# First attention: causal masks added by VectorE in PSUM, turned probabilities copied by ScalarE, next scores one filler block sooner

## The chip, the cores and the metric

The kernel runs on one core of one Trainium2 chip. The metric is device time in microseconds (us). The time before is the median of 3 runs. The shares, rows and durations come from one profiled execution of the kernel before.

## The reference

Two transformer blocks for one sequence of 512 tokens, width 1024, all in float32. The change touches the attention of the first block ("NSA", 8 heads of 64 dimensions, in 2 key groups). For each block of 128 queries it makes three masked softmaxes: over compressed keys, over selected blocks (at this length all 8 blocks of 64 keys are selected, so the mask is causal), and over a window of 512 (causal too). The three outputs are weighted by gates and added:

```python
s = jnp.einsum('qghd,qgnbd->qghnb', qi, ks) * scale
mask_s = sel_valid[..., None] & (kpos <= t[:, None, None, None])
p_s = masked_softmax(s.reshape(...), mask_s.reshape(...))
...
mask_w = ((wpos[None, :] >= 0) & (diff >= 0) & (diff < WINDOW))[:, None, None, :]
p_w = masked_softmax(s, mask_w)
...
o = g[..., 0:1] * o_c + g[..., 1:2] * o_s + g[..., 2:3] * o_w
```

Beside it the first block has a retention branch, whose input projections (`ret_in`, 16 tiles of 128 outputs) do not depend on the attention. Everything else (gates, merges, two feed-forward layers, a second attention, a state-space scan, cross attention) lies before or behind and is not changed.

## The kernel before

Each large product is `gemm(name, s, ...)`, one weight slot of 1024 rows by 128 outputs. An operand is split in a high and a low part, so each of the 8 row blocks k of a slot is three matmuls of 512 columns (line 1791): high by high, low activation by high weight, high activation by low weight. One such group of three is called a filler block here when it stands inside the attention. ScalarE makes the high part of a weight slot (`split_hi`, line 593), VectorE the low part (`split_lo`, line 1075), three slots ahead.

The attention is a loop over 16 units, u = 4p + i: p is a pair of heads, i a block of 128 queries, and the tile is 128 rows by (i+1)*128 keys, so units of i = 0, 1, 2, 3 have tiles of 128, 256, 384, 512 columns. The order on each engine is written out by hand, and engines meet by semaphores. For unit u:

- TensorE scores: banks 0 and 1 hold the selected branch of the two heads, banks 2 and 3 the window branch, bank 4 the compressed one (lines 1953, 1963). The mask is a matmul too: identity by the mask, added in PSUM to the last 128 columns of each bank (line 1956; line 1961 for the compressed branch).
- VectorE takes the row maxima (lines 1346 to 1354), ScalarE the exponentials (778 to 785), VectorE the sums, reciprocals, gate weights and the scaling of the probabilities (1365 to 1375).
- TensorE turns the scaled probabilities (line 1880 and 1987) into the same banks, runs 2 filler blocks of `ret_in` slot u, waits for the copy of the selected branch (`nsa_sel_t`), and scores unit u+1; between the selected and the window scores it waits for the copy of the window branch of unit u (`nsa_win_t`). Then come the products with the values (1999, 2002, 2004) and the 6 filler blocks that are left.
- The turned probabilities are copied from PSUM by ScalarE for the selected branch (line 790) and by VectorE for the window and the compressed branch (1379, 1381).
- In eight of the units (those of p = 1 and 2 with i = 0, 1, and all four of p = 3) VectorE also rotates a tile of the retention branch: `ret_rotate_halves` (1327, 1328) before it waits for the exponentials, `ret_rotate_sum` (1332, 1334) at the unit's end. ScalarE evacuates one `ret_in` tile in each unit from the second on (`ret_in_leaves`, line 771) and splits one weight slot.

Unit numbers below run from 0 to 15; a bank is one of the eight parts of PSUM.

Of the kernel before, what the change touches and what calls it, by code (L numbers as in the profile page):

```python
# [9 lines left out]
F32R = mybir.dt.float32r  # L10
ACT = mybir.ActivationFunctionType
ALU = mybir.AluOpType
AX = mybir.AxisListType.X

P = 128
S = 512
SC = S // P
D = 1024
DK = D // P
# [8 lines left out]
NSA_PAIRS = NSA_HEADS // 2  # L28
NSA_SCALE = DH ** -0.5
CMP_LEN, CMP_STRIDE, CMP_HIDDEN = 32, 16, 256  # L30
N_CMP = (S - CMP_LEN) // CMP_STRIDE + 1
# [166 lines left out]
def block_program(nc, xT, mem_t, w_all, params, consts, rope, decay, w_gate, w_dt, w1k, w1v, w2k, w2v, out_t):  # L198
    ctx = ExitStack()
    with ctx:  # L200
        sems = {}

        def sem(name):
            if name not in sems:
                sems[name] = ctx.enter_context(nc.semaphore(name))
            return sems[name]
# [22 lines left out]
        def place(name, shape, off, dt=F32):  # L229

            size = int(np.prod(shape[1:])) * 4
            assert arena0 + off * 1024 + size <= arena_end, (name, off, size, (arena_end - arena0) / 1024)
            return nc.alloc_sbuf_tensor_at(name, shape, dt, offset=arena0 + int(off * 1024))
# [5 lines left out]
        def const(name):  # L239
            return CO[:, CCOL[name][0]:CCOL[name][1]]  # L240

        ACC = [ctx.enter_context(nc.psum_tensor(f"acc{b}", [P, S], F32)) for b in range(2)]
        PS = [ctx.enter_context(nc.psum_tensor(f"bank{b}", [P, S], F32)) for b in range(6)]


        HH = place("act_hi", [P, DK, S], 0, F32R)
# [36 lines left out]
        IDR = place("ident_r", [P, P], 113.5, F32R)  # L283
        CAR = place("causal_r", [P, P], 114, F32R)
        CMR = place("cmp_mask_r", [P, SC * 32], 114.5, F32R)
# [297 lines left out]
        def _(act):  # L583
            A = nc.scalar.activation
# [167 lines left out]
            A(IDR[:], ident, ACT.Copy)  # L752
            A(CAR[:], const("causal"), ACT.Copy)
            A(CMR[:], const("cmp_mask"), ACT.Copy).then_inc(sem("nsa_masks"), 1)
# [18 lines left out]
            for p in range(NSA_PAIRS):  # L773
                for i in range(SC):
# [14 lines left out]
                    for hh in range(2):  # L789
                        ins = A(PTS[:, hh, 0:i + 1, :], PS[hh][:, 0:kw].rearrange("p (c t) -> p c t", t=P), ACT.Copy)  # L790
                    ins.then_inc(sem("nsa_sel_t"), 1)
                    if i:
                        ret_in_leaves(p, i - 1)
                    elif p:
                        act.wait_ge(sem("nsa_pv"), p * SC)
                        A(OA[:, p - 1, :], PS[5][:], ACT.Copy).then_inc(sem("nsa_out"), 1)
                        ret_in_leaves(p - 1, 3)
# [264 lines left out]
        def _(dve):  # L1062
# [273 lines left out]
            def rotated_at(p, i):  # L1336
# [3 lines left out]
                return (p - 1, i) if p and i < 2 else None  # L1340

            for p in range(NSA_PAIRS):
                for i in range(SC):
                    u, kw = p * SC + i, (i + 1) * P
                    dve.wait_ge(sem("nsa_sel_scored"), u + 1)
                    V.reduce_max(MX[:, 2:3], PS[0][:, 0:kw], AX)
                    chain.link(V.reduce_max(MX[:, 3:4], PS[1][:, 0:kw], AX))
                    TS(NM[:, 2:4], MX[:, 2:4], -NSA_SCALE, None, ALU.mult).then_inc(sem("nsa_sel_max"), 1)
                    dve.wait_ge(sem("nsa_win_scored"), u + 1)
                    V.reduce_max(MX[:, 0:2], PS[4][:, 0:64].rearrange("p (h c) -> p h c", h=2)[:, :, 0:N_CMP], AX)  # L1350
                    V.reduce_max(MX[:, 4:5], PS[2][:, 0:kw], AX)
# [5 lines left out]
                    turned = rotated_at(p, i)  # L1357
                    if turned:
                        ret_rotate_halves(*turned)

                    dve.wait_ge(sem("nsa_exp"), u + 1)
# [14 lines left out]
                        sem("nsa_win_scaled"), 1)  # L1376

                    dve.wait_ge(sem("nsa_win_turned"), u + 1)
                    V.tensor_copy(PTC[0:N_CMP], PS[4][0:N_CMP, P:3 * P].rearrange("p (h t) -> p h t", h=2))
                    for hh in range(2):  # L1380
                        ins = V.tensor_copy(PTW[:, hh, 0:i + 1, :], PS[2 + hh][:, 0:kw].rearrange("p (c t) -> p c t", t=P))
                    ins.then_inc(sem("nsa_win_t"), 1)
                    if turned:
# [374 lines left out]
        def _(pe):  # L1758
# [190 lines left out]
            def wide_scores(p, i, branch):  # L1949

                kw = (i + 1) * P
                for hh, rows in enumerate(head_rows):
                    MM(PS[2 * branch + hh][:, 0:kw], QK[rows, p, i * P:(i + 1) * P], QK[rows, 5 + branch, 0:kw], start=True,  # L1953
                       stop=False)
                for hh in range(2):
                    ins = MM(PS[2 * branch + hh][:, i * P:kw], IDR[:], CAR[:], start=False, stop=True)
                return ins
# [17 lines left out]
            for p in range(NSA_PAIRS):  # L1975
                for i in range(SC):
                    u, cols = p * SC + i, slice(i * P, (i + 1) * P)

                    pe.wait_ge(sem("nsa_sel_scaled"), u + 1)
# [8 lines left out]
                    ins.then_inc(sem("nsa_win_turned"), 1)  # L1988
                    gemm("ret_in", u, HH, HL, ks=range(0, 2))
                    pe.wait_ge(sem("nsa_sel_t"), u + 1)  # L1990
# [14 lines left out]
                    ins.then_inc(sem("nsa_pv"), 1)  # L2005
                    gemm("ret_in", u, HH, HL, ks=range(2, DK))

# [485 lines left out]
```

## Time and profile before

| what | value |
|---|---|
| median of 3 runs | 2032.09 us (2030.95 to 2032.53) |
| profiled execution | 2032.29 us, span of the trace 2030.6 us |
| TensorE busy over the span | 1981.5 us, 98% |
| VectorE busy | 1140.7 us, 56% |
| ScalarE busy | 812.5 us, 40% |
| attention loop, first score to last filler block | about 99.6 to 290.2 us of the span |

Times in rows count from the start of the span. A matmul row gives its start and its duration; durations overlap, since matmuls are pipelined, so what a matmul costs is the distance from its start to the next start. One float32 matmul stands as two records.

### The profile page before, as it was taken

What the parts mean: (1) busy time and instruction counts of PE and PEld (TensorE: products, weight loads), DVE (VectorE), ACT (ScalarE), POOL (GpSimd) and SP (SyncE); (2) the same over time, 40 slices, a digit from 0 to 9 for tenths busy, and PEclk for the clock granted to TensorE, in tenths of its full rate; (3) what the DMA queues carried; (4) which work ended last, traced back from release to release, by engine and by line L of the source; (5) the groups of instructions that cost most, each with busy time, mean ns of one, the idle gap of its engine ahead of it and who ended that gap; (6) DMA issues with size and microseconds to landing.
All of it is one profiled execution on the core that took longest, in us unless ns stands there. A gap on an engine that the chain in (4) does not pass through costs nothing.

```text
span 2030.6 us, 25955 instructions
## 1 busy us (share of the span) xinstructions
PE 1981.5 (98%) x10494; PEld 1607.2 (79%) x10494; DVE 1140.7 (56%) x1837; ACT 812.5 (40%) x1365; POOL 111.2 (5%) x131
## 2 busy tenths in 40 slices
PE   8999999999999999999999999999999999999997
PEld 6767767788888888888877777888889788888886
DVE  5567766644456444422627888796564465444323
ACT  4144432533344222222427777554435443222321
POOL 0000000000011000000200000331010020000000
PEclk9999999999999999999999999999999999999999
DMA  7111112233322333333222221113223223333331
GB/s 276 55 32 53 42 52 63 73 96 91 104 83 92 95 94 94 89 96 96 83 78 70 63 63 52 53 42 93 84 90 119 90 78 94 94 93 94 94 95 61
DMA packets 49431, 170.55 MB, mean 84 GB/s; under 512 B 5520, under 2 KB 8080, under 8 KB 48928
## 3 DMA queue, kind: packets, MB, share of 16 engines
q1 hardware_dynamic: 48816, 166.73, 27.4%
q0 software_dynamic: 496, 2.16, 0.3%
q8 instruction: 83, 1.36, 0.3%
q14 instruction: 36, 0.29, 0.0%
HBM read 166.77 MB, written 2.10 MB: 83 GB/s over the span
## 4 chain that ended last, share of the span: by engine, by line
PE 90%; DVE 7%; issue 1%; ACT 1%; DMA 0%; SPq 0%; DVEq 0%
PE acc L1791 57%; PE bank L1791 18%; PE bank L1880 2%; PE bank L1953 1%; PE bank L2092 1%; PE acc L2296 1%; DVE w_lo L1075 1%; PE bank L2127 1%; PE bank L2029 1%; DVE bank L1155 1%; PE bank L1926 1%; PE bank L2283 1%; PE bank L2317 1%; DVE residual L1161 1%; PE bank L1813 1%
## 5 line engine op out<-in xcount | busy, mean ns | idle before, releaser
L1075 DVE TENSOR_TENSOR w_lo<-w_raw,w_hi 128x1024 fp32r<-128x1024 f32 (+2 forms) x306 | 365.8, 1198 | 302.6 <-ACT w_hi L593 302.1
L1791 PE MATMUL acc<-act_hi,w_hi 128*128 128x512 f32 (+1 forms) x1160 | 457.5, 394 | 17.4 <-DVE w_lo L1075 9.7
L1791 PE MATMUL acc<-act_lo,w_hi 128*128 128x512 f32 (+1 forms) x1160 | 445.4, 384 | 0.0
L1791 PE MATMUL acc<-act_hi,w_lo 128*128 128x512 f32 (+1 forms) x1160 | 445.3, 384 | 0.0
L593 ACT ACTIVATE w_hi<-w_raw 128x1024 fp32r<-128x1024 f32 (+2 forms) x306 | 314.7, 1030 | 211.6 <-PE acc L1791 181.0
L1791 PEld LDWEIGHTS acc<-act_hi,w_hi 128*128 128x128 f32 x1160 | 218.9, 189 | 71.9 <-issue 16.3
L1791 PEld LDWEIGHTS acc<-act_hi,w_lo 128*128 128x128 f32 x1160 | 218.9, 189 | 47.0
L1791 PEld LDWEIGHTS acc<-act_lo,w_hi 128*128 128x128 f32 x1160 | 219.1, 189 | 45.7 <-issue 2.2
L1791 PE MATMUL bank<-act_hi,w_hi 128*128 128x512 f32 (+1 forms) x520 | 192.6, 370 | 1.2 <-DVE w_lo L1075 1.2
L1791 PE MATMUL bank<-act_lo,w_hi 128*128 128x512 f32 (+1 forms) x520 | 191.0, 367 | 0.0
L1791 PE MATMUL bank<-act_hi,w_lo 128*128 128x512 f32 (+1 forms) x520 | 191.0, 367 | 0.0
L1791 PE MATMUL acc<-ffn_hi,w_lo 128*128 128x512 f32 (+1 forms) x352 | 134.2, 381 | 0.0
L1791 PE MATMUL acc<-ffn_lo,w_hi 128*128 128x512 f32 (+1 forms) x352 | 134.2, 381 | 0.0
L1791 PE MATMUL acc<-ffn_hi,w_hi 128*128 128x512 f32 (+1 forms) x352 | 134.2, 381 | 0.0
L1791 PEld LDWEIGHTS bank<-act_hi,w_hi 128*128 128x128 f32 x520 | 97.8, 188 | 19.5 <-DVE w_lo L1075 1.4
L1791 PEld LDWEIGHTS bank<-act_lo,w_hi 128*128 128x128 f32 x520 | 97.8, 188 | 17.9 <-issue 0.2
L1791 PEld LDWEIGHTS bank<-act_hi,w_lo 128*128 128x128 f32 x520 | 97.8, 188 | 17.7
L617 ACT ACTIVATE ffn_hi<-product 128x512 fp32r<-128x512 f32 x44 | 27.8, 633 | 195.5 <-DVE product L1480 195.5
L1121 DVE TENSOR_TENSOR square_sum<-square_sum,evacuated 128x512 f32<-128x512 f32 (+1 forms) x47 | 31.1, 662 | 99.8 <-ACT evacuated L634 99.7
L1791 PEld LDWEIGHTS acc<-ffn_lo,w_hi 128*128 128x128 f32 x352 | 66.2, 188 | 14.2
L1791 PEld LDWEIGHTS acc<-ffn_hi,w_hi 128*128 128x128 f32 x352 | 66.2, 188 | 14.1
L1791 PEld LDWEIGHTS acc<-ffn_hi,w_lo 128*128 128x128 f32 x352 | 66.2, 188 | 13.9
(453 smaller groups left out, 3015.5 us busy)
## 6 DMA issues: line engine op xcount, KB each, us to landing
w_raw<-w_all SPq DMA_DIRECT2D x282, 512.0 KB, 3.6
w_raw<-w_all SPq DMA_DIRECT2D x16, 384.0 KB, 3.2
residual<-xT SPq DMA_DIRECT2D x8, 256.0 KB, 7.8
cmp_w_k<-w1k SPq DMA_DIRECT2D x1, 2048.0 KB, 8.3
cmp_w_v<-w1v SPq DMA_DIRECT2D x1, 2048.0 KB, 12.5
w_raw<-w_all SPq DMA_DIRECT2D x8, 256.0 KB, 2.6
out_t<-residual SPq DMA_DIRECT2D x16, 128.0 KB, 1.7
ret_decay<-decay POOLq DMA_DIRECT2D x4, 256.0 KB, 3.4
```

The lines of the kernel that those rows point to most:

```text
L593: A(WH[:, c % HI_RING, 0:nb * P], WR[:, c % RAW_RING, 0:nb * P], ACT.Copy).then_inc(s_hi, 1)
L617: A(dst, PR[:, j % 2, 0:n], ACT.Copy).then_inc(s_ph, 1)
L1075: TT(WL[:, c % RAW_RING, 0:nb * P], WR[:, c % RAW_RING, 0:nb * P], WH[:, c % HI_RING, 0:nb * P].bitcast(F32), ALU.subtract).then_inc(s_lo, 1)
L1121: TT(SSQ[:, cols], SSQ[:, cols], ev(name, m)[:, cols], ALU.add).then_inc(s_fsq, 1)
L1155: STT(out=scaled_at(k), in0=FO[:, k, cols], scalar=factor, in1=PS[(4, 3)[h]][:, cols], op0=ALU.mult, op1=ALU.mult).then_inc(sem("branch_sc ...
L1161: TT(X[:, k, cols], X[:, k, cols], scaled_at(k), ALU.add).then_inc(s_x, 1)
L1791: ins = MM(bank[:, cols], w[:, at, k * P:(k + 1) * P], x, start=first and r == 0 and k == 0, stop=last and r == 2 and k == nb - 1)
L1813: ins = MM(bank[:, c * P:(c + 1) * P], RC[:, c:c + 1].broadcast_to([P, P]), ident, start=True, stop=True)
L1880: ins = TR(PS[bank][:, to + c * P:to + (c + 1) * P], src[:, c * P:(c + 1) * P], ident)
L1926: ins = MM(PS[n][:, j * 2 * N_CMP:(j + 1) * 2 * N_CMP], W1[t][:, b, j * P:(j + 1) * P], BLK[t][:, b, :], start=b == 0, stop=b == 15)
L1953: MM(PS[2 * branch + hh][:, 0:kw], QK[rows, p, i * P:(i + 1) * P], QK[rows, 5 + branch, 0:kw], start=True, stop=False)
L2029: ins = MM(PS[3 + e][:, j * P:S], RVT[:, j, e * P:(e + 1) * P], RSM[:, j, 0:S - j * P], start=j == 0, stop=j == SC - 1)
```

## The change

Three things change. The four mask matmuls of each unit (line 1956) go, and with them the rounded copy of the mask; VectorE adds the mask to the last 128 columns of each of the four banks instead, two adds before the maxima of each branch. The copies of the turned window and compressed probabilities move from VectorE to ScalarE, right behind those of the selected branch. In the units with i below 3, the next scores begin after 1 filler block in place of 2 (i = 3: 2 as before, and 3 in the very last unit); the blocks behind them grow from 6 to 7. VectorE's rotation now stands as a whole at the end of the unit.

```diff
@@ act
             A(IDR[:], ident, ACT.Copy)
-            A(CAR[:], const("causal"), ACT.Copy)
@@
                     ins.then_inc(sem("nsa_sel_t"), 1)
+                    act.wait_ge(sem("nsa_win_turned"), u + 1)
+                    for hh in range(2):
+                        A(PTW[:, hh, 0:i + 1, :], PS[2 + hh][:, 0:kw].rearrange("p (c t) -> p c t", t=P), ACT.Copy)
+                    A(PTC[0:N_CMP], PS[4][0:N_CMP, P:3 * P].rearrange("p (h t) -> p h t", h=2), ACT.Copy).then_inc(
+                        sem("nsa_win_t"), 1)
                     if i:
                         ret_in_leaves(p, i - 1)
@@ dve
+            def hide_later(bank, i):
+
+                block = PS[bank][:, i * P:(i + 1) * P]
+                return TT(block, block, const("causal"), ALU.add)
+
             for p in range(NSA_PAIRS):
                 for i in range(SC):
                     u, kw = p * SC + i, (i + 1) * P
                     dve.wait_ge(sem("nsa_sel_scored"), u + 1)
+                    hide_later(0, i)
+                    chain.link(hide_later(1, i))
                     V.reduce_max(MX[:, 2:3], PS[0][:, 0:kw], AX)
...
                     dve.wait_ge(sem("nsa_win_scored"), u + 1)
+                    hide_later(2, i)
+                    chain.link(hide_later(3, i))
...
                     turned = rotated_at(p, i)
-                    if turned:
-                        ret_rotate_halves(*turned)
-
                     dve.wait_ge(sem("nsa_exp"), u + 1)
...
-                    dve.wait_ge(sem("nsa_win_turned"), u + 1)
-                    V.tensor_copy(PTC[0:N_CMP], PS[4][0:N_CMP, P:3 * P].rearrange("p (h t) -> p h t", h=2))
-                    for hh in range(2):
-                        ins = V.tensor_copy(PTW[:, hh, 0:i + 1, :], PS[2 + hh][:, 0:kw].rearrange("p (c t) -> p c t", t=P))
-                    ins.then_inc(sem("nsa_win_t"), 1)
+                    if turned:
+                        ret_rotate_halves(*turned)
                     if turned:
                         ret_rotate_sum(*turned)
@@ pe
                 for hh, rows in enumerate(head_rows):
-                    MM(PS[2 * branch + hh][:, 0:kw], QK[rows, p, i * P:(i + 1) * P], QK[rows, 5 + branch, 0:kw], start=True,
-                       stop=False)
-                for hh in range(2):
-                    ins = MM(PS[2 * branch + hh][:, i * P:kw], IDR[:], CAR[:], start=False, stop=True)
+                    ins = MM(PS[2 * branch + hh][:, 0:kw], QK[rows, p, i * P:(i + 1) * P], QK[rows, 5 + branch, 0:kw],
+                             start=True, stop=True)
                 return ins
@@
+                    lead = 1 if i < SC - 1 else 2 if p < NSA_PAIRS - 1 else 3
...
-                    gemm("ret_in", u, HH, HL, ks=range(0, 2))
+                    gemm("ret_in", u, HH, HL, ks=range(0, lead))
...
-                    gemm("ret_in", u, HH, HL, ks=range(2, DK))
+                    gemm("ret_in", u, HH, HL, ks=range(lead, DK))
```

TensorE at the end of unit 0's turning, in the kernel before: the last filler block ahead of unit 1's scores, those scores with their masks, and the first product with the values.

```order
L1791 MATMUL acc0<-act_hi_50,w_hi 128x512
L1791 MATMUL acc0<-act_lo_51,w_hi 128x512
L1791 MATMUL acc0<-act_hi_50,w_lo_49 128x512
L1953 MATMUL bank0<-nsa_qk_58 128x256
L1953 MATMUL bank1<-nsa_qk_58 128x256
L1956 MATMUL bank0<-causal_r_89,ident_r_88 128x128
L1956 MATMUL bank1<-causal_r_89,ident_r_88 128x128
L1953 MATMUL bank2<-nsa_qk_58 128x256
L1953 MATMUL bank3<-nsa_qk_58 128x256
L1956 MATMUL bank2<-causal_r_89,ident_r_88 128x128
L1956 MATMUL bank3<-causal_r_89,ident_r_88 128x128
L1961 MATMUL bank4<-cmp_mask_r_90,ident_r_88 128x64
```

The same place in the kernel after, from the turn of unit 0's compressed probabilities on.

```order
L1991 MATMUL bank4<-const_cols,cmp_probs_79 31x128 x2
L1796 MATMUL acc0<-act_hi_50,w_hi 128x512
L1796 MATMUL acc0<-act_lo_51,w_hi 128x512
L1796 MATMUL acc0<-act_hi_50,w_lo_49 128x512
L1958 MATMUL bank0<-nsa_qk_58 128x256
L1958 MATMUL bank1<-nsa_qk_58 128x256
L1958 MATMUL bank2<-nsa_qk_58 128x256
L1958 MATMUL bank3<-nsa_qk_58 128x256
L1964 MATMUL bank4<-cmp_mask_r_89,ident_r_88 128x64
L1966 MATMUL bank4<-cmp_keys_70,nsa_qk_58 128x64
```

The four mask matmuls are gone, and one filler block stands between the turning and the scores where two stood.

VectorE at the end of unit 4 (p = 1, i = 0) and the start of unit 5, in the kernel before: scaling, copies of the turned probabilities, the second half of the rotation, and the maxima.

```order
L1374 TENSOR_SCALAR nsa_probs_78<-nsa_probs_78,nsa_weights_87 128x128
L1375 TENSOR_TENSOR cmp_probs_79<-cmp_probs_79,nsa_weights_87 128x2x31
L1379 COPY cmp_probs_t_82<-bank4 31x256
L1381 COPY win_probs_t_81<-bank2 128x128
L1381 COPY win_probs_t_81<-bank3 128x128
L1332 TENSOR_TENSOR tmp_b_54<-evacuated,ret_rope_table_61 128x512
L1334 TENSOR_TENSOR ret_qk_94<-tmp_a_53,tmp_b_54 128x512
L1346 TENSOR_REDUCE nsa_max_83<-bank0 128x1
L1347 TENSOR_REDUCE nsa_max_83<-bank1 128x1
L1348 TENSOR_SCALAR nsa_neg_max_84<-nsa_max_83 128x2
L1350 TENSOR_REDUCE nsa_max_83<-bank4 128x2
```

The same place in the kernel after.

```order
L1384 TENSOR_TENSOR cmp_probs_79<-cmp_probs_79,nsa_weights_87 128x2x31
L1330 TENSOR_TENSOR tmp_a_53<-evacuated,ret_rope_table_61 64x512
L1331 TENSOR_TENSOR tmp_a_53<-evacuated,ret_rope_table_61 64x512
L1335 TENSOR_TENSOR tmp_b_54<-evacuated,ret_rope_table_61 128x512
L1337 TENSOR_TENSOR ret_qk_93<-tmp_a_53,tmp_b_54 128x512
L1348 TENSOR_TENSOR bank0<-bank0,const_cols 128x128
L1348 TENSOR_TENSOR bank1<-bank1,const_cols 128x128
L1356 TENSOR_REDUCE nsa_max_83<-bank0 128x1
L1357 TENSOR_REDUCE nsa_max_83<-bank1 128x1
L1358 TENSOR_SCALAR nsa_neg_max_84<-nsa_max_83 128x2
L1348 TENSOR_TENSOR bank2<-bank2,const_cols 128x128
L1348 TENSOR_TENSOR bank3<-bank3,const_cols 128x128
```

The three copies have left VectorE, all four operations of the rotation stand together behind the scaling, and each pair of maxima has two adds ahead of it.

ScalarE in unit 1 of the kernel after: the three copies stand between those of the selected branch and the evacuation of the `ret_in` tile.

```order
L788 ACTIVATE sel_probs_t_80<-bank0 128x256
L788 ACTIVATE sel_probs_t_80<-bank1 128x256
L792 ACTIVATE win_probs_t_81<-bank2 128x256
L792 ACTIVATE win_probs_t_81<-bank3 128x256
L793 ACTIVATE cmp_probs_t_82<-bank4 31x256
L769 ACTIVATE evacuated<-acc0 128x512
L592 ACTIVATE w_hi<-w_raw 128x1024
```

In the kernel before, the evacuation follows the two copies of the selected branch at once.

## Rows read from the trace of the kernel before

**Rows 1.** The page: busy time by engine, and the chain that ended last.

```profile
PE 1981.5 (98%) x10494; PEld 1607.2 (79%) x10494; DVE 1140.7 (56%) x1837; ACT 812.5 (40%) x1365; POOL 111.2 (5%) x131
PE 90%; DVE 7%; issue 1%; ACT 1%; DMA 0%; SPq 0%; DVEq 0%
```

**Rows 2.** Busy time by stretch; PEclk is TensorE's granted clock.

```profile
core 0: us, PE busy (x) PEld busy (x) DVE busy (x) ACT busy (x) POOL busy (x), PEclk, DMA share, GB/s
100.00:112.00 12.00, 8.16 (x35) 5.79 (x33) 4.67 (x23) 3.36 (x13) 0.00 (x0) 0.57 0.01 1
112.00:292.00 180.00, 177.84 (x1174) 132.38 (x1173) 129.44 (x364) 75.81 (x215) 0.70 (x1) 1.00 0.16 47
```

**Rows 3.** Timeline of TensorE, scores of unit 7: start us, us.

```profile
178.88 0.44 PE L1956 MATMUL bank<-causal_r,ident_r 128*128 128x128 f32 x2
179.25 1.13 PE L1953 MATMUL bank<-nsa_qk 64*128 64x512 f32 x4
180.31 0.44 PE L1956 MATMUL bank<-causal_r,ident_r 128*128 128x128 f32 x2
180.59 0.24 PE L1961 MATMUL bank<-cmp_mask_r,ident_r 128*128 128x64 f32 x1
```

**Rows 4.** Groups by shape, VectorE and ScalarE: count, busy us, mean ns.

```profile
L1556 DVE TENSOR_TENSOR bank<-bank,const_cols 128x256 f32<-128x256 f32 x24 | 8.7, 420 | 0.0
...
L1556 DVE TENSOR_TENSOR bank<-bank,const_cols 128x128 f32<-128x128 f32 x16 | 3.9, 289 | 0.0
```

**Rows 5.** Timeline of unit 7, VectorE, then TensorE's turn.

```profile
179.36 0.69 DVE L1346 TENSOR_REDUCE nsa_max<-bank 128x1 f32<-128x512 f32 x1 [1.48 <-PE bank L1956]
...
181.12 0.22 DVE L1350 TENSOR_REDUCE nsa_max<-bank 128x2 f32<-128x62 f32 x1 [0.27 <-PE bank L1963]
...
186.22 0.48 DVE L1372 TENSOR_SCALAR nsa_probs<-nsa_probs,nsa_weights 128x512 f32<-128x512 f32 x1
...
187.13 1.91 PE L1880 MATMUL bank<-const_cols,nsa_probs 128*128 128x128 f32 x16
```

**Rows 6.** Timeline of TensorE, turns of units 1 and 5.

```profile
118.10 1.04 PE L1880 MATMUL bank<-const_cols,nsa_probs 128*128 128x128 f32 x8
...
162.64 0.40 PE L1791 MATMUL acc<-act_lo,w_hi 128*128 128x512 f32 x1
162.87 0.40 PE L1791 MATMUL acc<-act_hi,w_lo 128*128 128x512 f32 x1
163.51 1.31 PE L1880 MATMUL bank<-const_cols,nsa_probs 128*128 128x128 f32 x8 [0.24 <-DVE nsa_probs L1372]
```

**Rows 7.** Timeline of unit 5, ScalarE and VectorE.

```profile
160.07 0.46 ACT L785 ACTIVATE cmp_probs<-bank,nsa_neg_max 128x31 f32<-128x31 f32 x2
...
160.28 0.69 DVE L1327 TENSOR_TENSOR tmp_a<-evacuated,ret_rope_table 64x512 f32<-64x512 f32 x1
...
160.98 0.69 DVE L1328 TENSOR_TENSOR tmp_a<-evacuated,ret_rope_table 64x512 f32<-64x512 f32 x1
...
161.70 0.22 DVE L1365 TENSOR_TENSOR cmp_probs<-cmp_probs,const_cols 128x62 f32<-128x62 f32 x1
```

**Rows 8.** Timeline of TensorE, turns and value product of the last units.

```profile
266.56 1.66 PE L1880 MATMUL bank<-const_cols,nsa_probs 128*128 128x128 f32 x12 [0.20 <-DVE nsa_probs L1372]
279.41 2.01 PE L1880 MATMUL bank<-const_cols,nsa_probs 128*128 128x128 f32 x16 [0.16 <-DVE nsa_probs L1372]
283.44 1.09 PE L1999 MATMUL bank<-sel_probs_t,sel_values 128*64 128x128 f32 x16 [0.38 <-DVE win_probs_t L1381]
```

**Rows 9.** Timeline, unit 0.

```profile
100.02 0.66 PE L1956 MATMUL bank<-causal_r,ident_r 128*128 128x128 f32 x2
100.61 0.80 PE L1953 MATMUL bank<-nsa_qk 64*128 64x128 f32 x4
...
101.33 0.69 PE L1956 MATMUL bank<-causal_r,ident_r 128*128 128x128 f32 x2
...
106.50 1.21 PE L1880 MATMUL bank<-const_cols,nsa_probs 128*128 128x128 f32 x4 [3.84 <-DVE nsa_probs L1372]
```

**Rows 10.** Timeline, end of units 7 and 5: copies, and the next maximum.

```profile
163.90 0.22 DVE L1375 TENSOR_TENSOR cmp_probs<-cmp_probs,nsa_weights 128x62 f32<-128x62 f32 x1
...
167.69 0.56 DVE L1346 TENSOR_REDUCE nsa_max<-bank 128x1 f32<-128x384 f32 x1 [0.20 <-PE bank L1956]
...
188.20 1.08 ACT L790 ACTIVATE sel_probs_t<-bank 128x512 f32<-128x512 f32 x2 [3.56 <-PE bank L1880]
```

More of the change, by code:

```diff
@@ L283, in block_program @@
         IDR = place("ident_r", [P, P], 113.5, F32R)
-        CAR = place("causal_r", [P, P], 114, F32R)
         CMR = place("cmp_mask_r", [P, SC * 32], 114.5, F32R)
```

## The prediction

> **What bounds the kernel now.** I read the page first. TensorE is busy 98% of the span and makes 90% of the chain that ended last, VectorE 7% [rows 1]. So a microsecond is saved where TensorE issues less or stops waiting, and a microsecond of VectorE counts only where TensorE waits for it. Then the stretches: in the attention loop behind its start TensorE is busy 177.84 of 180 us, at full clock, with VectorE at 129.44 and ScalarE at 75.81 [rows 2]. VectorE is the second engine, at 72%; ScalarE has room. In the first 12 us the granted clock is 0.57, so most of it is at 1.2 in place of 2.4 GHz. Last the timelines of single units, for what each part costs from start to start and for where TensorE stands still.
>
> **Part 1, the mask matmuls.** In unit 7 the selected pair starts at 178.88 and the next scores at 179.25: 0.37 us. The window pair starts at 180.31 and the next row at 180.59: 0.28 us [rows 3]. The mask pairs have 128 columns whatever the tile, so these two hold for all units; together 0.65. The 0.09 between the two is the way back from whole-array to half-array matmuls. The first pair disappears with its switches. Behind the second a whole-array matmul follows anyway (line 1961), which then meets the switch itself; for this I keep 0.05 of the 0.09 in the sum: 0.60 a unit, bounds 0.56 and 0.65. Units 1 to 15 are scored at full clock: 15 x 0.60 = 9.0 us (8.4 to 9.75). Unit 0 is counted in part 4. The Trainium skill (TensorE: Matmul & The Clock Gate, Back-to-back issue gap) has about 81 ns for a matmul of 128 columns with its weight load in a sustained stream; by that the 60 matmuls are worth 4.9 us and the whole would end 4.1 us later, near 2024; the rows here, with their switches, have 0.14 to 0.19 each, and I go by them.
>
> **Part 2, what the adds put on the path.** An add of a constant to 128 columns in PSUM stands in the trace in another stage at 289 ns [rows 4]; a second follows, by the 0.20 us spacing of the small operations, so a pair with its link (0.04) is 0.20 + 0.29 + 0.04 = 0.53 us, two pairs 1.06. The next larger form, 256 columns, has 420 ns: the upper bound, 0.79 a pair. Are they hidden? The cover is TensorE's work between the scores and the turn. Take unit 7, the widest tile. Window scores begin at 179.25, and the turn at 187.13 [rows 3, 5]: 7.88 us. After, that is 0.23 less (window masks) and one filler block more. A block is three matmuls at 0.23 [rows 6], 0.70, so 8.35. VectorE: from its first maximum at 179.36 to the end of the second scaling, 186.22 + 0.48 = 186.70, are 7.34 us [rows 5]. It grows by 1.06, and loses the 0.27 that it waited for the window scores: 8.13. With 0.11 ahead and 0.04 for the semaphore that is 8.28 against 8.35: slack 0.07, where it was 0.39. So the units with i = 3 just fit. The same subtraction gives 0.30 for i = 2 and 0.5 for i = 1; with i = 0 no block is gained, but the tile is the smallest and 1 us or more is left. I charge 0.1 us of waiting for each of the four widest units, 0.4 in all. Without the extra block each unit of i = 1 to 3 would stand worse by 0.70: that is what the earlier scores buy.
>
> **Part 3, the waits that go.** Unit 5 (i = 1, with rotation) turns at 163.51, 0.64 after the last filler matmul where the spacing is 0.23: 0.41 late; inside the turn it waits again, 1.31 against the 1.04 of unit 1, which has no rotation: 0.27 [rows 6]. Units 9 and 13 repeat it: 3 x 0.68 = 2.04. Unit 14 shows 0.20 idle, unit 15 0.16, and 0.17 of each wait is hidden in the length of the row (0.40 duration, 0.23 spacing): 0.37 and 0.33; with the waits inside the turn 0.56 and 0.43. Behind the last turn the value product waits 0.38 for VectorE's copies [rows 8]. Together 3.4 us. All of it comes from VectorE. The halves of the rotation, 0.70 each, lie between the exponentials, which end at 160.07 + 0.46 = 160.53, and the sums at 161.70 [rows 7]; behind the unit they free 1.13 us of path, so unit 5 has -0.41 + 1.13 + 0.47 - 0.68 = +0.5 slack (0.47: block less masks; 0.68: adds less the idle before the window maximum). The copies of the last unit go to ScalarE.
>
> What is late next? The rotation, now four operations of about 0.70, 2.8 us, between the last scaling and the next scores. In unit 5 that gap is from 163.90 + 0.22 to 167.69, 3.57 us [rows 10]; it loses a block (0.70) and the selected masks (0.37), and gains 0.5 since the turn no longer waits, less the 0.27: 2.7. So VectorE is late by some 0.1 us there, which the 0.3 of unit 6 takes. In units 4, 8 and 12 (i = 0) and behind unit 14 TensorE comes to the next scores later against VectorE's last scaling, so more is left. ScalarE: in unit 7 its two copies end at 188.20 + 1.08 = 189.28, as the turned window is ready; two more (1.08) and the small one (bound by one wide copy, 0.6; I take 0.35) end near 190.7, and the window scores of unit 8 stand behind two blocks (1.40) and the first scores (about 0.4, half of the 0.72 at half clock in unit 0), from 187.13 + 1.91 = 189.04: 190.9 [rows 5, 9, 10]. Slack 0.2. With narrower tiles the copies shrink as fast as the turn. Behind them on ScalarE are the evacuation and the split for slot u+3, later by about 1.4 us; VectorE's split that needs it stands behind the next unit's window maxima, and the accumulator is wanted a unit later. TensorE's weight slots are used in the same order, so SyncE's loads and the decay table's load on GpSimd only move along with them; DMA is at 16% [rows 2].
>
> **Part 4, unit 0.** At half clock the mask pairs take 100.61 - 100.02 = 0.59 and about 0.49, and the turn waits at 106.50 [rows 9]. TensorE is idle there, so only the path counts: window scores ready 1.08 sooner, adds 0.53 more, and VectorE busy with the selected branch until then; 0.46 us sooner. Work issued in that gap runs at half clock as long as the slow stretch lasts, so 0.25 of it is kept (0 to 0.46).
>
> **Sum.** 9.0 + 3.4 + 0.25 - 0.4 = 12.2 us. The profiled execution took 2032.29 us, 1.7 more than its span, and gives 2020.1; the median is 0.2 lower: **2019.9 us**. Its own range has 8.4 to 9.75 for the masks, 2.5 to 3.5 for the waits, and 0 to 2 for new waits: 2018.3 to 2022.
>
> **The rivals.**
> *The adds are dearer* (chance 0.15). At the price of the 256-column form each unit's path grows by 0.52 more: i = 3 waits 0.45, i = 2 0.22, times four is 2.7, and the rotating units, already level, add about 1. The time is 2023.6. For it: between filler blocks VectorE would be busy almost without a pause in units 5, 9, 13 to 15. Against: the row of the same shape.
> *A longer slow stretch* (0.06). TensorE's idle gap in unit 0 begins a microsecond earlier and ends half a microsecond earlier, so it is longer. If the clock came back later by as much again as the slow stretch lasts now (0.57 over 12 us is 10.3 us at half rate), 5.1 us are lost: 2025.0. Against: the same work follows as before, sooner. The Trainium skill (TensorE: Matmul & The Clock Gate, HAM oscillation — how this bites in real kernels) says that idle gaps between bursts of matmuls put the clock back to half rate, so a longer gap speaks for this rival; the trace agrees that the gap and the slow stretch lie together.
> *Hardly any change* (0.05): masks at the low price and three waits of 0.1 to 0.5 us in every four units, within 4.1 us of before, about 2028.5.
> *Slower* (0.04): VectorE becomes the bound. TensorE's slack over four units is about 0.07 + 0.3 + 0.5 + 1.4 = 2.3 us; 12.2 us lost over four rounds are 3.05 each, so the path must grow by (3.05 + 2.3) / 4 = 1.3 a unit, 0.33 an add: from 0.53 us an add in place of 0.20 the gain is gone, and from 0.6 the kernel is slower by over 0.2%, 2037 at 0.62. For it: VectorE would write to PSUM while TensorE writes to it and ScalarE reads it, and each add would have to suffer as much. Against: the add at 289 ns stands in a stage where those two work as well.
>
> **How the numbers follow.** The forecast has 0.70. A measurement tells about 0.2% (4.1 us) from no change. Above 2025.5 I leave about 0.1, below 2018.3 about 0.06; so 2018.3 to 2025.5. Faster: 0.70 + 0.15 + 0.06 is 0.91, I take 0.90; same 0.06; slower 0.04.
>
> **What would show it.** Scores to scores without a gap, 0.6 us a unit less on TensorE; adds at 0.29; no wait of TensorE at the turns with i = 1 and 2, some hundredths at i = 3; the window scores never waiting for ScalarE; VectorE late for the maxima behind units 5, 9 and 13 by 0.1. Turns late by more than 0.3 at i = 3, or a clock below 0.57 in the first 12 us, would make it wrong.

## The result and the profile after

The changed kernel takes 2017.62 us (median of 4 runs, 2016.59 to 2019.11) against 2032.31 us for the kernel before (4 runs, 2030.95 to 2032.83): ratio 0.9931, 95% interval 0.9918 to 0.9944. It is 14.7 us faster, where 12.2 were forecast, and the time lies 0.7 us below the range (2018.3 to 2025.5).

The page of the kernel after, its busy times and its chain, answers to [rows 1].

```profile
PE 1967.8 (98%) x10430; PEld 1599.1 (79%) x10430; DVE 1136.9 (56%) x1853; ACT 828.9 (41%) x1412; POOL 111.3 (6%) x131
...
PE 92%; DVE 6%; issue 1%; ACT 1%; DMA 0%; SPq 0%; DVEq 0%
```

TensorE is busy 13.7 us less over the span. Its share of the chain that ended last rose from 90 to 92%, and VectorE's fell from 7 to 6%. Busy time by stretch in the kernel after, columns as in [rows 2]:

```profile
100.00:112.00 12.00, 7.62 (x39) 5.20 (x38) 6.71 (x32) 4.99 (x20) 0.00 (x0) 0.60 0.01 1
112.00:275.00 163.00, 163.00 (x1092) 123.24 (x1090) 122.65 (x370) 89.56 (x256) 0.70 (x1) 1.00 0.17 51
275.00:400.00 125.00, 123.36 (x515) 92.47 (x515) 78.41 (x102) 45.29 (x67) 1.62 (x3) 1.00 0.24 70
```

The loop ends 15 us sooner, and by these rows TensorE is busy in all of it (some waits don't show in them, see below). The slow stretch is as long as before: from 97 to 112 us, which holds the whole of it in both traces, the granted clock is 0.66 before and after, about 10.2 us at half rate. It begins and ends some 0.6 us sooner, and so the window from 100 us on reads 0.60 where it read 0.57. Behind the loop nothing moved: from the first matmul that turns retention values (290.86 before, 275.81 after) to the end of the span are 1739.7 and 1740.1 us.

Where the time came from, by the starts of TensorE's rows in both traces:

| stretch | before | after | gained |
|---|---|---|---|
| start of the span to the first scores | 99.60 | 99.20 | 0.40 |
| first scores to the turn of unit 1 | 18.50 | 17.26 | 1.24 |
| turn of unit 1 to the first turned retention value | 172.76 | 159.35 | 13.41 |
| from there to the end | 1739.7 | 1740.1 | -0.4 |

The first and the last row cancel. The edit changes only one thing in them, the copy of the mask on ScalarE ahead of the first scores, and with that copy back (e1 below) the first scores start at 99.16. Over the fourteen traces told of here the first scores start between 98.8 and 99.9 and the last stretch takes 1739.7 to 1741.0, so about half a microsecond either way is what any one trace has of its own. In the two longest last stretches (e10 and e11) the clock falls to half for 6.8 us near 1246 us, where the other traces have 3.4 us in that part of the kernel.

TensorE in unit 7 of the kernel after, timeline, from the last filler matmul to the value products; [rows 3] are the same unit before.

```profile
170.89 0.40 PE L1796 MATMUL acc<-act_hi,w_lo 128*128 128x512 f32 x1
171.22 1.99 PE L1958 MATMUL bank<-nsa_qk 64*128 64x512 f32 x8
173.13 0.30 PE L1964 MATMUL bank<-cmp_mask_r,ident_r 128*128 128x64 f32 x1
173.27 0.41 PE L1966 MATMUL bank<-cmp_keys,nsa_qk 128*128 128x64 f32 x2
173.61 0.66 PE L2003 MATMUL bank<-sel_probs_t,sel_values 128*64 128x128 f32 x8
```

And the same unit before, a few rows around those shown ahead:

```profile
174.81 1.47 PE L1880 MATMUL bank<-const_cols,nsa_probs 128*128 128x128 f32 x12
...
176.26 0.47 PE L1791 MATMUL acc<-act_hi,w_hi 128*128 128x512 f32 x1
...
177.83 1.13 PE L1953 MATMUL bank<-nsa_qk 64*128 64x512 f32 x4
...
180.67 0.41 PE L1963 MATMUL bank<-cmp_keys,nsa_qk 128*128 128x64 f32 x2
181.01 0.33 PE L1999 MATMUL bank<-sel_probs_t,sel_values 128*64 128x128 f32 x2
```

From the first score to the first value product: 181.01 - 177.83 = 3.18 us before, 173.61 - 171.22 = 2.39 after. That is 0.79, not 0.60. The scores row alone shows where the difference lies: from the first of its eight records to the next row are 173.13 - 171.22 = 1.91 us, where before each group of four took 1.05 (177.83 to 178.88) and again 1.06, and 1.91 is 0.2 less than the two. The same 0.79 holds for every tile width in the loop: 1.91 to 1.12 where the unit scored has i = 0, 2.76 to 1.97 at i = 2. (One float32 score product is two passes, a record each, and the records of the two heads start 0.01 us apart; so eight records are four passes, with two heads in each.)

The turns of units 6 and 7 after, timeline of TensorE:

```profile
168.48 0.40 PE L1796 MATMUL acc<-act_hi,w_lo 128*128 128x512 f32 x1
168.71 1.65 PE L1885 MATMUL bank<-const_cols,nsa_probs 128*128 128x128 f32 x12
...
170.34 0.48 PE L1796 MATMUL acc<-act_hi,w_hi 128*128 128x512 f32 x1
...
180.21 0.40 PE L1796 MATMUL acc<-act_hi,w_lo 128*128 128x512 f32 x1
180.50 2.02 PE L1885 MATMUL bank<-const_cols,nsa_probs 128*128 128x128 f32 x16
...
182.49 0.48 PE L1796 MATMUL acc<-act_hi,w_hi 128*128 128x512 f32 x1
```

No row shows idle time, and still TensorE waits a little. A turn with i = 2, from its first record to the next filler matmul, takes 1.45 us when nothing is late (unit 6 before: 176.26 - 174.81); here it is 170.34 - 168.71 = 1.63, 0.18 more. With i = 3 it takes 1.88; here it begins 0.06 late (0.29 behind the last filler matmul, where 0.23 is the spacing) and takes 1.99, 0.11 more. Read this way, over units 1 to 15, the waits at the turns are 1.22 us after and 3.04 before, and before the last value product waited 0.45 more.

### The profile page after: what moved, and what is told of

The parts are those of the page before. It is cut to its first block, busy times and chain, and to the rows that moved or that the text cites. A ratio compares the mean times of both kernels' runs of the same rounds, so it can differ in the third digit from the quotient of the medians.

```text
span 2015.9 us, 25890 instructions
## 1 busy us (share of the span) xinstructions
PE 1967.8 (98%) x10430; PEld 1599.1 (79%) x10430; DVE 1136.9 (56%) x1853; ACT 828.9 (41%) x1412; POOL 111.3 (6%) x131
## 4 chain that ended last, share of the span: by engine, by line
PE 92%; DVE 6%; issue 1%; ACT 1%; DMA 0%; SPq 0%; DVEq 0%
PE acc L1796 58%; PE bank L1796 18%; PE bank L1885 2%; PE bank L2096 1%; PE acc L2300 1%; PE bank L1958 1%; PE bank L2131 1%; PE bank L2033 1%; DVE bank L1158 1%; PE bank L1931 1%; DVE w_lo L1078 1%; PE bank L2287 1%; PE bank L2321 1%; DVE residual L1164 1%; PE bank L1818 1%
## 5 line engine op out<-in xcount | busy, mean ns | idle before, releaser
L852 ACT ACTIVATE evacuated<-evacuated 128x512 f32<-128x512 f32 x44 | 27.9, 633 | 121.3 <-DVE evacuated L1479 121.3
```

The costliest lines, as they stand in the source:

```text
L852: A(ev(up, t), ev(up, t), ACT.Silu).then_inc(sem("gate_made"), 1)
```

## The experiments

The method for all of them: the loop is measured from the turn of unit 1 to the first turned retention value, waits are turns that begin or end later than the same turn without a wait, and "score stage" is the distance from the first score of a unit with i = 2 to the value product that follows. The kernel before was measured beside each group of kernels again: 2031.7 us with e1 to e4, 2031.9 with e5 to e8, 2032.6 with e9 to e12; the ratios go by these.

| kernel | median us | loop us | waits at turns us | score stage us |
|---|---|---|---|---|
| before | 2032.3 | 172.76 | 3.04 | 2.76 |
| after | 2017.6 | 159.35 | 1.22 | 1.97 |
| all masks on TensorE (e1) | 2029.2 | 169.26 | 0 | 2.76 |
| selected masks on TensorE (e2) | 2024.0 | 166.12 | 0 | 2.54 |
| window masks on TensorE (e3) | 2019.3 | 161.31 | 0 | 2.19 |
| no masks (e4) | 2016.0 | 158.27 | 0 | 1.97 |
| adds alone (e5) | 2030.7 | 172.68 | 13.56 | 1.97 |
| lead of two blocks (e6) | 2024.6 | 166.68 | 8.53 | 1.97 |
| rotation split (e7) | 2021.6 | 163.56 | 5.36 | 1.97 |
| copies on VectorE (e8) | 2036.9 | 175.75 | 16.30 | 1.97 |
| after again (e9) | 2018.2 | 159.33 | 1.16 | 1.97 |
| no compressed mask (e10) | 2016.9 | 159.01 | 2.30 | 1.86 |
| two matmuls ahead (e11) | 2016.5 | 158.28 | 0 | 1.97 |
| both (e12) | 2015.6 | 157.27 | 0.61 | 1.86 |

**What the mask matmuls cost: e1, e2, e3.** In the changed kernel, mask matmuls are put back for both branches, for the selected one, or for the window one, and VectorE's adds for them go.

```diff
                     ins = MM(PS[2 * branch + hh][:, 0:kw], ...,
-                             start=True, stop=True)
+                             start=True, stop=not (branch == 0))
+                if branch == 0:
+                    for hh in range(2):
+                        ins = MM(PS[2 * branch + hh][:, i * P:kw], IDR[:], CAR[:], start=False, stop=True)
@@ dve
-                    hide_later(0, i)
-                    chain.link(hide_later(1, i))
```

(Shown for e2; e1 has `branch in (0, 1)` and no adds, e3 `branch == 1` and no adds to banks 2 and 3. ScalarE's rounded copy of the mask comes back in all three.)

> The changed kernel with all four mask matmuls back on TensorE and no adds on VectorE. Theory S (switches): in the trace of the kernel after, scores to the next product took 0.79 us less per unit than before, because the two middle passes of the scores stand 0.32 apart in place of 0.42 once no whole-array matmul lies between the branches; the masks then cost 15 x 0.79 = 11.9 us, the waits at the turns with i = 2 and 3 (about 1.3 us in the kernel after) vanish, and the time is near 2017.6 + 10.6 = 2028.2. Rival P (the prediction's size, 0.60 a unit, the rest of the gain from elsewhere): 2017.6 + 9.0 - 1.3 = 2025.3.

> The changed kernel with the mask matmuls of the selected branch alone back on TensorE; VectorE adds only the window masks. Theory S: the selected pair costs its own 0.36 and 0.1 on each of the two passes beside it, 0.57 a unit, 8.6 us, less the waits of 1.3: 2024.9, with passes 0.42 apart again in both branches. Rival P: 0.37 a unit, 5.6 less 1.3: 2021.9, passes stay 0.32 apart.

> The changed kernel with the mask matmuls of the window branch alone back on TensorE. Both theories have 0.23 a unit for this pair (a whole-array matmul follows anyway): 3.4 us less the waits of 1.3, 2019.7. Theory S adds that the middle passes stay at 0.32; if they go to 0.42 here, and not with the selected masks, S is wrong.

Measured: 2029.17 us (ratio to before 0.9987, interval 0.9977 to 0.9996), 2024.04 (0.9964, 0.9951 to 0.9977) and 2019.28 (0.9936, 0.9921 to 0.995). Theory S had 2028.2, 2024.9 and 2019.7, at most 1.0 off; rival P was 3.9 us off for e1 and 2.1 for e2. Unit 7 of e2, timeline of TensorE:

```profile
174.53 1.13 PE L1958 MATMUL bank<-nsa_qk 64*128 64x512 f32 x4
175.59 0.44 PE L1962 MATMUL bank<-causal_r,ident_r 128*128 128x128 f32 x2
175.96 1.13 PE L1958 MATMUL bank<-nsa_qk 64*128 64x512 f32 x4
177.02 0.30 PE L1967 MATMUL bank<-cmp_mask_r,ident_r 128*128 128x64 f32 x1
177.15 0.41 PE L1969 MATMUL bank<-cmp_keys,nsa_qk 128*128 128x64 f32 x2
```

Unit 7 of e3, the same view:

```profile
172.70 1.99 PE L1958 MATMUL bank<-nsa_qk 64*128 64x512 f32 x8
174.62 0.44 PE L1962 MATMUL bank<-causal_r,ident_r 128*128 128x128 f32 x2
174.89 0.25 PE L1967 MATMUL bank<-cmp_mask_r,ident_r 128*128 128x64 f32 x1
174.97 0.41 PE L1969 MATMUL bank<-cmp_keys,nsa_qk 128*128 128x64 f32 x2
```

Compare the distance from the first score to the product with the compressed keys: 2.05 us in the kernel after (173.27 - 171.22), 2.62 in e2, 2.27 in e3. The selected pair costs 0.57, the window pair 0.22, and 0.79 are both. The same two matmuls of 128 columns are 2.6 times dearer in the one place. In e2 the scores stand in two groups of 1.06 us, in e3 in one of 1.92. Between the two score groups the pair brings its own 0.37, and it also breaks up a row of four passes over the same half-array layout, of which the two in the middle then take 0.1 more each. e1 has no waits at the turns either, so the waits of before are gone by the other parts of the change, with the masks still on TensorE.

**What the adds cost: e4.** The four adds are taken out of the changed kernel and nothing stands in their place.

```diff
-                    hide_later(0, i)
-                    chain.link(hide_later(1, i))
...
-                    hide_later(2, i)
-                    chain.link(hide_later(3, i))
```

> The changed kernel without the four adds and without mask matmuls: the causal mask of the selected and the window branch is left out of the computation, the rest is the same. It prices the adds on the path. Theory S: TensorE waits about 1.3 us in the loop at the turns with i = 2 and 3 and some 0.5 us of unit 0's gap belong to the adds: 2016.0. Rival D (the adds are hidden everywhere): 2017.6, no change. Rival E (VectorE still sets much of the loop): 2013 or lower.

This kernel leaves the causal mask of two branches out, so it prices the adds and is no version to use. Measured: 2015.99 us (0.992, 0.9905 to 0.9934), as theory S had it. The loop is 1.08 us shorter and all waits at the turns are gone; from the first scores to the turn of unit 1 another 0.38 is saved (17.26 to 16.88). That is the whole price, some 1.5 us, of 64 adds of 0.29 us each, 15.8 us of VectorE's time:

```profile
L1348 DVE TENSOR_TENSOR bank<-bank,const_cols 128x128 f32<-128x128 f32 x64 | 15.8, 293 | 27.5 <-PE bank L1958 27.4
```

(This is the group by shape of the kernel after.) They are hidden but for 1.1 us in the loop and 0.4 ahead of it.

**What hides the adds: e5 to e8.** e5 is the kernel before with the mask edit alone. e6, e7 and e8 each undo one other part of the changed kernel.

```diff
@@ e6
-                    lead = 1 if i < SC - 1 else 2 if p < NSA_PAIRS - 1 else 3
+                    lead = 2
@@ e7
                     turned = rotated_at(p, i)
+                    if turned:
+                        ret_rotate_halves(*turned)
                     dve.wait_ge(sem("nsa_exp"), u + 1)
...
-                    if turned:
-                        ret_rotate_halves(*turned)
                     if turned:
                         ret_rotate_sum(*turned)
@@ e8, dve (and the three copies of act go)
+                    dve.wait_ge(sem("nsa_win_turned"), u + 1)
+                    V.tensor_copy(PTC[0:N_CMP], ...)
+                    for hh in range(2):
+                        ins = V.tensor_copy(PTW[:, hh, 0:i + 1, :], ...)
+                    ins.then_inc(sem("nsa_win_t"), 1)
                     if turned:
                         ret_rotate_halves(*turned)
```

> The kernel before with the masks moved to VectorE and nothing else of the change. Theory H (the other edits are what hides the adds): TensorE issues 11.9 us less, but the adds lengthen VectorE's path by 1.06 in every unit where the slack was 0.4 to 0.7, and in the rotating units there was none; from the slacks the waits grow by 10 to 12 us, so the time is 2030 to 2033. Rival A (the parts add up): 2032.3 - 11.9 + 2 = 2022.

> The changed kernel with 2 filler blocks ahead of the scores in every unit, as before. Theory H: in each of the eleven units with i = 1 to 3 whose scores now come one block earlier the cover falls by 0.70 us against slacks of 0.0 to 0.5: waits of 0.2 to 0.8, together 6 to 8 us, 2023.5 to 2025.5. Rival A: the slack of VectorE is enough, 2017.6 to 2018.5.

> The changed kernel with the halves of the rotation back ahead of the wait for the exponentials. Theory H: 1.1 us of path come back in units 5, 9, 13 (slack 0.5), 14 and 15 (slack 0.1 to 0.3) and none in the four with i = 0: waits of 0.6 to 0.9 in five units, 3 to 4 us, 2020.6 to 2021.6. Rival A: 2017.6.

> The changed kernel with the copies of the turned window and compressed probabilities back on VectorE, ahead of the rotation. Theory H: VectorE has to wait for the turn before it may rotate, and in the rotating units it is then 2 us late for the next maxima; from the slacks 12 to 15 us are lost, 2030 to 2033, all in the units with rotation, next to nothing in units 1 to 4 and 7 to 8. Rival A (VectorE is busy 75% of the loop and has room for 1.1 us a unit): 2018 to 2020.

Measured: e5 2030.66 us (0.9992, 0.9983 to 1.0002), e6 2024.61 (0.9959, 0.9944 to 0.9974), e7 2021.58 (0.9944, 0.9929 to 0.9959), e8 2036.89 (1.0021, 1.0012 to 1.0031). Theory H holds in e5, e6 and e7; in e8 its mechanism shows, but the median is 4 us beyond its range. Rival A is out by 4 to 17 us. What TensorE waited for in the loop by the list of waits, the largest row of each, with total, times and longest (it counts idle time alone); first e5, then e6, e7 and e8:

```profile
PE bank L1887 <- DVE nsa_probs L1379: 9.4, 11, 1.4
```

```profile
PE bank L1885 <- DVE nsa_probs L1381: 3.8, 8, 0.6
```

```profile
PE bank L1885 <- DVE nsa_probs L1383: 2.8, 5, 0.6
```

```profile
PE bank L1885 <- DVE nsa_probs L1376: 12.4, 7, 2.0
```

In e5 the turns of units 5, 9, 13, 14 and 15 are 1.7 us late each, the others with i = 3 0.9, with i = 2 0.7 to 0.8, and the sum is 13.6 us. Of these 3.0 were there before; the 10.5 that are new eat nearly all of the 11.1 that TensorE saves in the loop. In e6 every turn with i = 1, 2, 3 is late, by 0.57, 0.71 and 0.86. In e7 five turns are, beside the 0.16 at i = 3 that the changed kernel has too: 1.0 in units 5, 9, 13, 0.93 in 14, 0.88 in 15. In e8 they are those of units 5, 6, 9, 10, 13, 14 and 15, by 1.9 to 3.1; the others, 0.16 at most.

The 3.1 of unit 14 in e8 is not waiting alone:

```profile
266.22 2.33 PE L1885 MATMUL bank<-const_cols,nsa_probs 128*128 128x128 f32 x12 [1.96 <-DVE nsa_probs L1376]
```

(timeline of TensorE). In this trace the granted clock falls to half once inside the loop, from 266.9 us on for 3.4 us (0.72 over 266 to 272), and the turn takes 2.4 us where 1.64 is usual; TensorE had been busy 9.26 of the 11 us before 266. No other trace here has this. The traced execution is the fastest of ten, 2033.84 us at a mean clock of 0.994, 0.8 above theory H's range; the other nine took 2035.1 to 2037.9 at 0.991 to 0.993. More stretches at half clock in them would account for the rest, but that is not shown, since they left no trace.

So no part gains in proportion to what it takes off an engine; each counts by the turns at which VectorE is late.

**What is left: e9 to e12.** e10 takes out the last mask matmul. e11 moves the boundary by one matmul instead of a block of three; `gemm` gets a range of single matmuls (`steps`).

```diff
@@ e10
-                MM(PS[4][:, 0:64], IDR[:], CMR[:, i * 32:(i + 1) * 32]..., start=True, stop=False)
-                return MM(PS[4][:, 0:64], QK[:, p, i * P:(i + 1) * P], ..., start=False, stop=True)
+                return MM(PS[4][:, 0:64], QK[:, p, i * P:(i + 1) * P], ..., start=True, stop=True)
@@ e11
-                    lead = 1 if i < SC - 1 else 2 if p < NSA_PAIRS - 1 else 3
+                    lead = 2 if i < SC - 1 else 6 if p < NSA_PAIRS - 1 else 9
-                    gemm("ret_in", u, HH, HL, ks=range(0, lead))
+                    gemm("ret_in", u, HH, HL, steps=(0, lead))
-                    gemm("ret_in", u, HH, HL, ks=range(lead, DK))
+                    gemm("ret_in", u, HH, HL, steps=(lead, 3 * DK))
```

In e10 and e12 the maximum of the compressed branch goes over all keys, masked ones too; the exponentials are multiplied by the 0/1 mask as before. It is a bound from above, which keeps its accuracy as long as no masked score lies far above the others.

> The changed kernel itself once more, on the same chip as the next three. Both theories: 2017.6 within 1 us of the earlier median; turns with i = 3 late by 0.17 and those behind units 5, 9, 13 by 0.18 again.

> The changed kernel without the mask matmul of the compressed branch. The maximum is then taken over all compressed keys; the probabilities are multiplied by the 0/1 mask afterwards as before. Theory S: this matmul is the one that meets the way back to the whole array behind the window scores (0.13 to the next start, where 0.08 stood when the window masks were ahead of it), and the next one inherits the switch: 0.08 a unit, 1.2 us. Rival P (it costs its whole distance): 0.13 a unit, 2.0 us. In the trace the first product with the compressed keys then shows 0.19 (S) or 0.14 (P) to its second pass.

> The changed kernel with two filler matmuls ahead of the scores in place of a whole block of three, in units with i below 3: 0.23 us more cover behind them. Theory H: the waits at the turns, 1.2 us in the loop, go, and ScalarE's copies still arrive (the window copies with at most 0.1 to spare at i = 1): 1.0 to 1.2 us faster than the changed kernel. Rival W (the copies come late): the window scores wait 0.1 to 0.2 a unit and the gain is nil or a loss.

> Both edits together: no mask matmul of the compressed branch, and two filler matmuls ahead of the scores. Theory: they add, 1.2 + 1.1 = 2.3 us faster than the changed kernel, 2015.3. Rival W: the copies are the next limit and only one of the two counts.

Measured, on one chip: e9 2018.21 us (2017.06 to 2019.06; ratio to before 0.9931, 0.9919 to 0.9944), e10 2016.87 (2016.09 to 2018.31; 0.9926, 0.9914 to 0.9938), e11 2016.45 (2016.26 to 2017.6; 0.9924, 0.9912 to 0.9937), e12 2015.62 (2015.14 to 2017.25; 0.9921, 0.9908 to 0.9935). The medians are too close for a verdict between neighbours; the loops in the traces are not: 159.33, 159.01, 158.28, 157.27.

Unit 7 of e10, timeline of TensorE:

```profile
171.00 1.99 PE L1958 MATMUL bank<-nsa_qk 64*128 64x512 f32 x8
172.92 0.43 PE L1964 MATMUL bank<-cmp_keys,nsa_qk 128*128 128x64 f32 x2
173.29 0.88 PE L2001 MATMUL bank<-sel_probs_t,sel_values 128*64 128x128 f32 x12
```

From first score to value product 2.29 in place of 2.39: 0.11 a unit at i = 2 (0.10 here), between the 0.08 and the 0.13 of the two theories. The product's own first pass takes 0.16 to the second, where it took 0.14: some 0.02 of a switch is inherited, not 0.05. Of the 1.6 us that 15 units save, 1.1 come back as waits (1.16 to 2.30), since VectorE's path starts at the selected scores, which are not sooner, and its cover is 0.1 shorter; its loop gains 0.32. In e11 every wait at a turn is gone, 1.05 us, and no window score waits for ScalarE, so rival W is out. With both, the loop is 2.06 us shorter than in e9, and 0.6 of waits are left. That is less than the 2.3 expected, and more than 0.32 and 1.05 together: the two matmuls take up 1.7 of the 2.3 that e10 waits. e12 is the fastest version here, 2.6 us by the medians under the changed kernel on the same chip.

## Why the prediction was wrong, step by step

**What bounds the loop** was right: every kernel's loop is TensorE's own work and what it waits at the turns. The loop of e1 (no adds, no waits) less that of e4 (no masks, no waits) is 10.99 us, 14 score stages at 0.79 = 11.06.

**Part 1 failed in size, and by it the time fell below the range.** The step is "together 0.65 ... 0.60 a unit, bounds 0.56 and 0.65", and with it "15 x 0.60 = 9.0 us". It measured 0.79 a unit, 11.1 us in the 14 units scored in the loop and 11.9 if unit 1 is counted alike, and the upper bound, 9.75, was below it. It took the distance from the mask pair to the next row as all that the pair costs. e2 and e3 show what stands in its place: the window pair costs 0.22, as that step had it (0.23), and the selected pair 0.57, where it had 0.37, because it lies between two groups of half-array matmuls and the two passes beside it take 0.1 longer each, inside the score rows. The rows shown ahead already had the length of those score groups; I did not ask what they would be without a break. This one step is 2.9 us (2.7 in the loop alone), more than the whole error of 2.5; the waits of part 2 offset 0.8 of it.

The four mask matmuls of a unit took 0.79 us here, 0.20 each. The figure of the Trainium skill (TensorE: Matmul & The Clock Gate, Back-to-back issue gap), about 81 ns in a sustained stream, would have been further off than mine.

**Part 2 was right in mechanism and too cheap.** The adds cost 293 ns, as the row of the same shape said, and almost all are hidden. I charged 0.4 us of waits; there are 1.22: 0.17 in each of the four units with i = 3 (0.1 was charged), and 0.18, 0.16 and 0.18 behind the rotation in units 6, 10 and 14, where I had VectorE 0.1 late and 0.3 of slack. The subtraction went to the start of the turn alone. In unit 7 that start is 0.06 late where 0.07 of slack was forecast, 0.13 off. The rest is lost inside the turn, which waits a second time, for the scalings of the window branch: 0.11 in unit 7 and all 0.18 in unit 6, whose turn begins on time (168.71 - 168.48 = 0.23). Of these 0.18, 0.13 stand at that second wait, where two starts are 0.19 and 0.16 apart instead of 0.11. The sum had no term for that.

**Part 3 was right.** The waits of before were 3.49 us (3.04 at the turns, 0.45 at the last value product; 3.4 forecast), and all are gone, in e1 as well, where there are no adds. e7 and e8 show that with the adds in place both the moved rotation and ScalarE's copies are needed for it; what either would do without the adds no run shows. ScalarE is in time: the copies end at 184.11 in unit 7,

```profile
181.63 1.09 ACT L788 ACTIVATE sel_probs_t<-bank 128x512 f32<-128x512 f32 x2 [3.25 <-PE bank L1885]
182.78 1.09 ACT L792 ACTIVATE win_probs_t<-bank 128x512 f32<-128x512 f32 x2
183.75 0.36 ACT L793 ACTIVATE cmp_probs_t<-bank 31x256 f32<-31x256 f32 x1
```

with 0.36 us for the small one (0.35 forecast), and the window scores, some 0.3 us behind the first at 184.06, start without a gap.

**Part 4**: the stretch from the first scores to the turn of unit 1 is 1.24 us shorter; with 0.79 taken for unit 1's masks, as in the loop, 0.45 is left for unit 0 where 0.25 was taken, within its bounds. This 0.45 is a remainder and not a reading. What the rows show is that the turn of unit 0 comes 0.68 us sooner after the first scores (6.22 in place of 6.90), where 0.46 was forecast; the terms given for that, 1.08 less 0.53, make 0.55, and 0.46 can't be worked out from them. The other 0.56 is gained behind that turn. There unit 1's scores now begin at 108.26, inside the slow stretch, where they began at 110.51, behind it. So its stage fell from 2.33 to 2.24 us only, against 1.54 in unit 5 at full clock, and the filler block that ran at half clock in its place, 1.30 us, now runs at full clock, 0.70.

The sum for the loop, where every term is read from rows: 14 x 0.79 + 3.49 - 1.22 = 13.3, against 13.41 from the stretches. With unit 1's 0.79 and the remainder it is 11.85 + 3.49 - 1.22 + 0.45 = 14.6, where the forecast had 9.0 + 3.4 - 0.4 + 0.25. The slow end of the forecast's own range, 2022, does not follow from its bounds either: 8.4 + 2.5 - 2 is 8.9 us less, about 2023.2.

**The rivals.** The adds are not dearer than their row (293 against 289 ns). The slow stretch did not grow: it lasts about 10.2 us in both traces, though TensorE's gap in it grew from 3.84 to 4.38 us,

```profile
105.42 1.21 PE L1885 MATMUL bank<-const_cols,nsa_probs 128*128 128x128 f32 x4 [4.38 <-DVE nsa_probs L1381]
```

(timeline of the kernel after, unit 0). The stretch ends 3.8 us behind the turn of unit 0 before and 4.3 behind it after, so half a microsecond more of work ran at half clock, some 0.25 us, an estimate, of the 0.68 that the turn came sooner. The rule of the Trainium skill on idle gaps (TensorE: Matmul & The Clock Gate, HAM oscillation — how this bites in real kernels), which spoke for that rival, did not show here as a later return of the clock.

The slower outcome, VectorE as the bound, is real as a mechanism: e8 is there, at 2036.9 (2033.8 in its trace), by leaving 1 us of copies a unit on VectorE. It needed no dearer adds.

## What to carry to other kernels

- A small matmul between two groups of half-array matmuls costs its own distance and what it does to its neighbours. Ask what the rows beside it would look like without it, and look in the trace for an uninterrupted group; where an add or a multiply by a mask can go elsewhere, take the one first that breaks such a group.
- Work moved to a second engine is free only at the places where the first engine arrives later than it. Write the slack of each unit down, since a part that gains nothing alone (e5) counts together with the others, and ask of every wait inside a stage, not only of the one at its start.
- Waits below the difference between a row's duration and its spacing (0.40 and 0.23 here) show no idle time. Compare the distance between starts with that of a unit that does not wait.

## What the runs showed of the hardware

- Passes of float32 matmuls on half the rows, two heads at a time, stand 0.42 us apart at 384 columns right behind a switch from whole-array matmuls or ahead of one, and 0.32 in an uninterrupted group (unit 6, kernel after against before; a pass is one record of each head). At 512 columns the four passes of a unit take 1.91 to 1.92 us together (kernel after, e3) and 2.11 to 2.12 in two groups (before, e2). The difference is 0.1 a pass at 128 columns too (0.21 and 0.11, unit 8).
- A pair of float32r matmuls of 128 columns costs TensorE 0.57 us between two such groups and 0.22 in front of another whole-array matmul. The cause inside the engine is not settled: the runs show where the 0.1 a pass goes, not why.
- In all fourteen traces TensorE's clock falls to half near the first scores, from 0.3 us ahead of the first to 1.6 behind it, and stays there for about 10.2 us, with 3.84 us of idle TensorE in it (before) as with 4.38 (after).
- VectorE's add of 128 columns from PSUM to PSUM took 0.293 us, in a loop where TensorE writes PSUM and ScalarE reads it too, against 0.289 in the stage where it stood before.
